# Squares of x in the first section of a four-part trunk kernel: who computes them, who adds them, and when the tiles of x are requested

## The reference, cut to what matters

```python
def rms_norm(x, g):
    xf = x.astype(jnp.float32)
    y = xf * lax.rsqrt(jnp.mean(xf * xf, axis=-1, keepdims=True) + EPS)
    return (y * g.astype(jnp.float32)).astype(x.dtype)

hnorm = rms_norm(x, mixer_norm[layer])
qkv = (hnorm @ w_in).astype(jnp.float32)
```

## Time and profile before

| | us |
|---|---|
| median of three runs | 3263.97 |
| lowest and highest | 3261.46 and 3265.09 |
| the profiled execution's own time | 3262.6 |
| its span | 3260.8 |
| PE busy | 3116.1 (96% of the span) |
| DVE, ACT, POOL busy | 1292.6, 1104.6, 927.5 |

### The profile page before, as it was taken

The page is one execution under the profiler, slowest core; times in us unless marked ns, Lnnn a source line. Parts: engine busy times, 40 slices in busy tenths (PEclk is TensorE's granted clock), DMA queues, the critical chain, the costliest instruction groups (busy, mean ns, idle before and its releaser), DMA issues. The chain is left out here.

```text
span 3260.8 us, 44365 instructions
## 1 busy us (share of the span) xinstructions
PE 3116.1 (96%) x16134; PEld 2692.2 (83%) x16134; DVE 1292.6 (40%) x3508; ACT 1104.6 (34%) x3122; POOL 927.5 (28%) x787
## 2 busy tenths in 40 slices
PE   6999999999999968999999999999788999999999
PEld 5999999999999956788888887778566788888887
DVE  5455555565555553422213133520263422213131
ACT  3555556555555543211111123111263211111110
POOL 5444444444444312222222222122202222222221
PEclk9999999999999978999999999999898999999999
DMA  3222222232222214111111111111111111111112
GB/s 123 60 66 81 76 77 77 70 86 65 82 76 75 62 39 168 43 48 48 50 48 50 46 52 46 39 46 55 62 40 52 46 52 46 52 46 52 46 52 78
DMA packets 143125, 201.85 MB, mean 62 GB/s; under 512 B 29611, under 2 KB 109118, under 8 KB 142910
## 3 DMA queue, kind: packets, MB, share of 16 engines
q1 hardware_dynamic: 140606, 194.81, 18.7%
q10 hardware_dynamic: 2304, 4.20, 0.3%
HBM read 173.25 MB, written 25.70 MB: 61 GB/s over the span
## 5 line engine op out<-in xcount | busy, mean ns | idle before, releaser
L69 PE MATMUL ps_qk<-w_hi,attn_hT_hi 128*128 128x384 f32 x1536 | 539.8, 351 | 25.1 <-POOL w_lo L847 13.1
L71 PE MATMUL ps_qk<-w_hi,attn_hT_lo 128*128 128x384 f32 x1536 | 516.7, 336 | 0.0
L70 PE MATMUL ps_qk<-w_lo,attn_hT_hi 128*128 128x384 f32 x1536 | 516.5, 336 | 0.0
L924 POOL TENSOR_TENSOR first_w_lo<-first_raw,first_w_hi 128x1024 fp32r<-128x1024 f32 x96 | 231.3, 2409 | 855.4 <-ACT first_w_hi L920 855.4
L924 POOL TENSOR_TENSOR second_w_lo<-second_raw,second_w_hi 128x1024 fp32r<-128x1024 f32 x72 | 172.1, 2391 | 620.1 <-ACT second_w_hi L920 620.1
L69 PEld LDWEIGHTS ps_qk<-w_hi,attn_hT_hi 128*128 128x128 f32 x1536 | 289.3, 188 | 47.6 <-DVE attn_hT_lo L658 25.6
L70 PEld LDWEIGHTS ps_qk<-w_lo,attn_hT_hi 128*128 128x128 f32 x1536 | 290.3, 189 | 0.0
L71 PEld LDWEIGHTS ps_qk<-w_hi,attn_hT_lo 128*128 128x128 f32 x1536 | 289.7, 189 | 0.0
L69 PE MATMUL first_ps<-first_hid_hi,first_w_hi 128*128 128x512 f32 x640 | 250.6, 392 | 33.3 <-DVE first_hid_lo L1250 33.3
L888 POOL TENSOR_TENSOR rs<-var,minus_half 128x4 f32<-128x4 f32 x192 | 193.2, 1006 | 289.5 <-DVE var L736 289.4
L69 PE MATMUL first_ps<-first_hT_hi,first_w_hi 128*128 128x512 f32 x640 | 252.7, 395 | 14.2 <-POOL first_w_lo L924 14.2
(11 more groups left out here) (258 smaller groups left out, 6130.1 us busy)
## 6 DMA issues: line engine op xcount, KB each, us to landing
raw<-in_wqkv SPq DMA_DIRECT2D x192, 192.0 KB, 2.4
first_raw<-in_w SPq DMA_DIRECT2D x64, 512.0 KB, 3.2
second_raw<-in_w SPq DMA_DIRECT2D x64, 512.0 KB, 3.2
v_dram<-v_out SPq DMA_DIRECT2D x192, 64.0 KB, 1.5
w_bc<-share_dram SPq DMA_DIRECT2D x48, 256.0 KB, 4.4
v_raw<-v_dram SPq DMA_DIRECT2D x32, 256.0 KB, 3.0
first_raw<-in_vo_pieces SPq DMA_DIRECT2D x16, 512.0 KB, 3.2
bias<-bias_dram SPq DMA_DIRECT2D x16, 256.0 KB, 3.4
```

What stands on the lines that cost most here:

```text
L69: pe.matmul(out, a_hi, b_hi, start=first, stop=False)
L70: pe.matmul(out, a_hi, b_lo, start=False, stop=False)
L71: return pe.matmul(out, a_lo, b_hi, start=False, stop=last)
L924: pool.tensor_tensor(self.lo[:, n % 2, :], self.raw[:, n % self.RAW, :], self.hi[:, n % 2, :].bitcast(F32), ALU.subtract).then_inc(self.lo ...
```

## The change

GpSimd no longer squares: the squares of odd k move to DVE, those of even k stay on ACT. Nobody adds squares: PE takes each square tile into the mean columns by itself, eight matmuls of one column for each k that accumulate in PSUM over k. The columns of k-1 are issued behind P k in T = 0, those of k = 7 at the start of T = 1. The squares lie in three buffers in turn (`total` and the two `shared`). SP requests all tiles of x before the first request that waits.

```diff
-        squares = [total[:]] + [shared[k % 2][:].rearrange("p g x -> p (g x)")[:, 0:SEQ] for k in range(1, KT)]
+        square_slots = [total[:]] + [b[:].rearrange("p g x -> p (g x)")[:, 0:SEQ] for b in shared]
...
             for n in range(TT):
                 sp.dma_start(x_tiles[n], x_dram[n * P:(n + 1) * P, :]).then_inc(x_in[n], 16)
-                if n >= 4:
-                    sp.wait_ge(w_lo_done, n - 3)
+                if n < 4:
+                    sp.dma_start(raw[:, n % 4], wqkv[n]).then_inc(raw_in[n % 4], 16)
+            for n in range(4, TT):
+                sp.wait_ge(w_lo_done, n - 3)
                 sp.dma_start(raw[:, n % 4], wqkv[n]).then_inc(raw_in[n % 4], 16)
...
-            sp.wait_ge(summed, KT - 1)
+            sp.wait_ge(summed, KT)
             sp.dma_start(hot, onehot.rearrange("g b x -> b g x")).then_inc(hot_in, 16)
...
+                        if T == 0 and k >= 1:
+                            mean_columns(k - 1)
...
                 if T == 1:
-                    products(range(KT // 2))
-                    means()
-                    products(range(KT // 2, KT))
+                    mean_columns(KT - 1)
+                    products(range(KT))
                     turn_tiles()
...
-            def means():
-                pe.wait_ge(summed, KT - 1)
-                pe.wait_ge(unit_set, 1)
+            def mean_columns(k):
+                if k == 0:
+                    pe.wait_ge(unit_set, 1)
+                if k % 2 == 0:
+                    pe.wait_ge(even_squared, k // 2 + 1)
+                else:
+                    pe.wait_ge(odd_squared, k // 2 + 1)
                 for t in range(TT):
-                    mm = pe.matmul(ps_mean[:, t:t + 1], total[:, t * P:(t + 1) * P], ones[:, 0:1], start=True, stop=True)
-                mm.then_inc(mean_mm, 1)
+                    mm = pe.matmul(ps_mean[:, t:t + 1], square_slots[k % 3][:, t * P:(t + 1) * P], ones[:, 0:1],
+                                   start=k == 0 and t == 0, stop=k == KT - 1 and t == TT - 1)
+                mm.then_inc(summed, 1)
...
-                    act.activation(squares[k], x_tiles[k], ACT.Square).then_inc(even_squared, 1)
+                    act.activation(square_slots[k % 3], x_tiles[k], ACT.Square).then_inc(even_squared, 1)
...
-                if k >= 2:
-                    add_squares(k - 1)
-            add_squares(KT - 1)
+                if k % 2 == 1:
+                    if k >= 3:
+                        dve.wait_ge(summed, k - 2)
+                    dve.tensor_tensor(square_slots[k % 3], x_tiles[k], x_tiles[k], ALU.mult).then_inc(odd_squared, 1)
...
             def means():
-                dve.wait_ge(mean_mm, 1)
+                dve.wait_ge(summed, KT)
...
                 lo_part(k % 4, 0, k)
-                if k % 2 == 1:
-                    pool.wait_ge(x_in[k], 16)
-                    if k >= 3:
-                        pool.wait_ge(summed, k - 2)
-                    pool.tensor_tensor(squares[k], x_tiles[k], x_tiles[k], ALU.mult).then_inc(odd_squared, 1)
```

More of the change, by code:

```diff
@@ L237, in attention_phase @@
         even_squared, odd_squared, summed = sem("even_squared"), sem("odd_squared"), sem("summed")
-        mean_mm, mean_done, root_done = sem("mean_mm"), sem("mean_done"), sem("root_done")
+        mean_done, root_done = sem("mean_done"), sem("root_done")
         rel_in, hot_in, filled, zeroed, unit_set = sem("rel_in"), sem("hot_in"), sem("filled"), sem("zeroed"), sem("unit_set")
@@ L642, in _ @@
             dve.memset(rel[REL_BUCKETS:REL_BUCKETS + 1, :], MASKED).then_inc(filled, 1)
[L644 to L653, removed]
             dve.wait_ge(norm_in, 16)
```

## The result

The changed kernel takes 3272.38 us (median of 8 runs, 3268.92 to 3274.91), the kernel before 3263.53 beside it: a ratio of 1.0028, with a 95% interval of 1.0019 to 1.0038. It is slower by 8.9 us, near the 3272 of the forecast. The profiled execution is the quickest of the eight, 3268.92 us with a span of 3266.7, 5.9 us more than the span of before.

What follows compares the result with a forecast made beforehand. DVE and POOL bound T = 0 before; afterwards PE would, with eight 3.4 us sets and six 1.1 us products, 33.8 us. T = 2 moves from 44.2 to 53.2, +9.0 us, giving 3272 us, range 3262 to 3277 (0.82).

Steps and rivals of the forecast that it cites:

- What bounds the fill: T = 0: DVE and POOL bind it, PE waits; without their squares and sums, data of k = 7 could come by 31.
- The price of a set at the low clock: Mean columns on PE in T = 0: 16 matmuls at 0.213 us, 3.4 us a set, with 1.7 and 3.7 as ends.
- the second rival: PE in T = 0: a set costs no more at the low clock than at the high; T = 2 at 40.3, 3259; chance 0.05.
- The first rival: PE in T = 0: unbroken work brings 2.4 GHz early, at 16; T = 2 at 36.4, -7.8, 3255 us; chance 0.09.
- T = 1: After set 7 at 46.9: 24 matmuls, quickening after 4.2 us, take 6.1 us; T = 2 starts at 53.2.
- The wait for `qkn`: PE's 1.39 us wait in T = 1 goes, already inside the sum.
- What was costed at nothing: T = 0: square waits, x tiles ahead of weight piece 4, and later SP loads hide behind PE's slowness, margins 4 to 6 us.
- The mark: Start of P 0 of T = 2, at 44.22 before; forecast at 53.2, +9.0 us.

Runs made afterwards that it cites:

- the 128-column version: Changed kernel with each float32 mean matmul streaming 128 columns of ones instead of one, into two PSUM banks; 3255.3 us, a second time 3256.4 us.
- the one with POOL's squares: Changed kernel with the odd squares moved back from DVE to POOL; 3269.6 us in one run.
- one matmul of eight: Changed kernel leaving out seven of the eight mean matmuls in each of the seven early sets, all waits kept; 3257.2 us, ratio 0.9979.
- loads in turns: Changed kernel with only the load order undone, x tile k and weight piece k requested in turns as before; 3274.6 us in one run.
- the array kept at work: The 128-column version with load requests in turns, plus 20 extra matmuls before P 0 and 5 between P 0 and P 1; 3253.9 us, ratio 0.9976.
- before with DVE's squares: Kernel before with only the odd squares moved from POOL to DVE, which still adds them all; 3262.2 us, ratio 0.9999.

## Why the prediction was right

- **What bounds the fill.** Confirmed from both sides: with the sets all but gone the data bring P 7 at 27.75 (I had said they could be there by 31), and taking the squares from POOL to DVE in the old kernel brought it 1.6 us forward.
- **The price of a set at the low clock** carried the sum. I took 3.4 us from a doubling of the high-clock set. The pace inside a set is that, 0.213 us; a set behind a product takes 3.26, since its first distance is short, and set 7 takes 3.42. A k is 4.37 us for my 4.5. Its lower bound, the second rival, is out: the set's time halved when the clock doubled, as the 128-column version shows in one trace (3.27, then 1.70).
- **The clock.** The first rival was that a PE at work without a pause brings 2.4 GHz. From 13.0 to 50.2 PE and its loads were busy for all of 37.2 us, the product matmuls took 0.52 us each and started 0.32 apart, and the shorter distances came at 50.3 only, in T = 1, as the forecast had it. The Trainium skill, "TensorE: Matmul & The Clock Gate", section "What's actually happening", has the gate follow how busy the array was. By the busy time of PE's records this trace does not agree; what the runs show is that the level stayed low with sets of 1 and 64 columns and rose with float32 sets of 128.
- **T = 1.** Set 7 ended at 46.3 (46.9 foretold), the quick distances came 4.0 us later (4.2), T = 2 at 52.57 (53.2). The mark moved by 8.35 us, not 9.0: seven sets behind a product were 0.14 us shorter each, and all of this execution's fill began 0.3 later.
- **The wait for `qkn`** is gone, as said.
- **What was costed at nothing.** The squares' waits were there, 4.8 and 3.7 us on ACT, and cost nothing; weight piece 4 made ACT wait 1.8 us at 17.0, as foretold, and undoing the order moved nothing.

The mechanism and the mark were right. That the median came within half a us of the number is luck: the remainder behind T = 2 varies by 6 us from one execution to another, and the profiled execution itself is only 5.9 us longer in span than the one of before, with a mark 8.35 later.

## What to carry to other kernels

Here a matmul of one column cost what one of 64 or 128 columns did, and half as many loads cost half: count loads, at the clock that the array will have there, and not columns. To sum over a tile with the tile as the stationary operand is cheap once (1.7 us) and dear eight times, above all in a fill where PE is at 1.2 GHz (3.3 us each). Before idle slots of PE are filled with such work, look at which level the clock has there; if the sets must stay, try them wider: up to 128 columns cost no time here, and with 128 float32 columns the level rose.

## What was not expected

- A load of 128 columns of 4-byte weights sets a pace of 0.213 us at the low clock, with 2 or 128 fp32r columns behind it as with 1, 64 or 128 of float32. The Trainium skill, "TensorE: Matmul & The Clock Gate", section "LDWEIGHTS (loading the stationary operand)", gives a load's time in ns as columns / 1.2 and names no level of the clock: an estimate of 0.107 us. At the high level the set of before agrees (0.112 us apart); at the low level the measured value is twice the page's, and the measurement decides.
- PE stood at the low level for 37 us while no gap was left in its records. Busy time was no sign of the clock here.
- The remainder of the span behind T = 2, with the same code, varies between 3214.1 and 3220.0 us. The mean granted clock over the span goes with it at the ends, though not strictly: 0.980 where it is least (the changed kernel, and the one with POOL's squares), 0.978 in three of the four where it is most (one matmul of eight, loads in turns, the array kept at work), but 0.979 in the fourth (before with DVE's squares, 3219.8). A stretch around the mLSTM phase, busy time by stretch, first of the changed kernel, then of the same with its loads in turns:

```profile
2300.00:2620.00 320.00, 261.34 (x1170) 208.35 (x1169) 141.65 (x343) 115.78 (x237) 58.53 (x43) 0.93 0.14 47
```

```profile
2300.00:2620.00 320.00, 263.25 (x1160) 209.08 (x1159) 139.80 (x340) 115.84 (x236) 56.99 (x44) 0.91 0.14 47
```

Both kernels start T = 2 within 0.04 us of each other, and the spans end 5.8 us apart, so this arises on the way, and not all in the stretch shown: the first matmul into `mc_ps_s` starts at 2345.36 in one and 2348.33 in the other, 3.0 us apart already, and `second_ps` is first written at 2468.48 and 2471.49, still 3.0 apart. The rest comes behind that. What decides it was not tried.
